# Second output projection in column halves, with the router and half of the first gather issued under and behind it; two small tables turned elsewhere

## The reference

```
h = rms_norm(x);  q,k,v,qi,ki,wi,pool,gate_a,gate_p = split(h @ w_in)      # 1024 x 3652
attn = top-64 sparse attention chosen by the indexer (qi, ki, wi), rotary, softmax
pooled = multi-scale trailing means minus identity, mixed per group, scaled
merged = sigmoid(gate_a) * (attn @ w_branch_attn) + sigmoid(gate_p) * (pooled @ w_branch_pool)
x = x + merged @ w_out
h2 = rms_norm(x);  logits = h2 @ router_w + router_b;  top 4 of 32 experts, softmax over the four
x = x + sum over chosen experts of gate * (swiglu(h2 @ w_gate_up[e] + b_gate_up[e]) @ w_down[e] + b_down[e])
```

## Time and profile before

| | |
|---|---|
| time, three runs | 1159.08, 1159.86, 1162.68 us; median 1159.86 |
| the profiled execution | 1162.73 us, its span 1160.8 us |
| PE busy | 1061.9 us (91%) |
| DVE, ACT busy | 291.2 us (25%), 117.4 us (10%) |
| DMA | 430.31 MB, mean 371 GB/s |

### The profile page before, as it was taken

The page is one execution under the profiler, slowest core; times in us unless marked ns, Lnnn a source line. Parts: engine busy times, 40 slices in busy tenths (PEclk is TensorE's granted clock), DMA queues, the critical chain, the costliest instruction groups (busy, mean ns, idle before and its releaser), DMA issues.

```text
span 1160.8 us, 12090 instructions
## 1 busy us (share of the span) xinstructions
PE 1061.9 (91%) x4830; PEld 442.6 (38%) x4830; DVE 291.2 (25%) x594; ACT 117.4 (10%) x208; POOL 5.2 (0%) x12
## 2 busy tenths in 40 slices
PE   7999999899999998989899999999999999999996
PEld 4544545543434342424243333333333333334332
DVE  2563121322222222121212122222222222222222
ACT  2124201110000101010100000000000000000000
POOL 1000000000000000000000000000000000000000
PEclk9899999899999999999999999999999999999999
DMA  9932475357999999999999999999999999999994
GB/s 348 340 141 73 167 278 206 137 235 298 430 427 427 431 427 430 427 430 428 429 429 427 430 427 430 427 429 429 427 430 427 430 427 430 428 429 429 427 423 184
DMA packets 39984, 430.31 MB, mean 371 GB/s; under 512 B 4880, under 2 KB 5008, under 8 KB 15392
## 3 DMA queue, kind: packets, MB, share of 16 engines
q1 hardware_dynamic: 39136, 428.11, 88.3%
q0 software_dynamic: 544, 1.90, 0.5%
q10 hardware_dynamic: 288, 0.08, 0.0%
HBM read 429.03 MB, written 1.05 MB: 370 GB/s over the span
## 4 chain that ended last, share of the span: by engine, by line
PE 65%; DMA 29%; DVE 3%; issue 1%; SPq 1%; ACT 0%; DVEq 0%
DMA slot<-w_gate_up_dram 28%; PE bank L1110 24%; PE bank L1135 11%; PE bank L862 9%; PE bank L1055 6%; PE bank L1084 5%; PE bank L889 5%; PE bank L1124 2%; DVE x L790 2%; PE bank L837 1%; PE bank L1095 1%; DMA slot<-w_down_dram 1%; PE bank L1026 0%; SPq L255 0%; DMA consts<-consts_dram 0%
## 5 line engine op out<-in xcount | busy, mean ns | idle before, releaser
L1110 PE MATMUL bank<-slot,scr 128*64 128x512 f32 x2048 | 461.6, 598 | 29.9 <-DMA slot<-w_gate_up_dram 29.9
L1110 PEld LDWEIGHTS bank<-slot,scr 128*64 128x64 f32 x2048 | 142.1, 137 | 319.6 <-issue 265.6
L1135 PE MATMUL bank<-slot,scr 128*64 128x512 f32 x1024 | 234.6, 600 | 20.3 <-DMA slot<-w_down_dram 19.2
L765 DVE COPY scr<-bank 128x512 f32<-128x512 f32 x32 | 22.1, 692 | 462.4 <-PE bank L1110 462.4
L1135 PEld LDWEIGHTS bank<-slot,scr 128*64 128x64 f32 x1024 | 69.8, 137 | 159.4 <-issue 120.8
L862 PE MATMUL bank<-slot,scr 128*128 128x512 f32 (+1 forms) x256 | 106.6, 578 | 2.1 <-DVE g L514 0.9
L1084 PE MATMUL bank<-scr 64*128 64x512 f32 x256 | 63.6, 613 | 24.3 <-DVE x L790 23.4
L790 DVE TENSOR_TENSOR x<-bank,x 128x512 f32<-128x512 f32 x68 | 44.0, 687 | 130.4 <-PE bank L1084 128.2
L862 PEld LDWEIGHTS bank<-slot,scr 128*128 128x128 f32 x256 | 48.3, 204 | 55.4 <-issue 53.2
L771 DVE TENSOR_TENSOR scr<-bank,bgu 128x512 f32<-128x512 f32 x64 | 41.2, 686 | 111.3 <-PE bank L1124 111.3
L1055 PEld LDWEIGHTS bank<-scr,xn 128*128 128x128 f32 x512 | 62.8, 199 | 13.2 <-issue 13.2
(11 more groups left out here) (166 smaller groups left out, 356.7 us busy)
## 6 DMA issues: line engine op xcount, KB each, us to landing
slot<-w_gate_up_dram SPq DMA_DIRECT2D x128, 2048.0 KB, 32.8
slot<-w_down_dram SPq DMA_DIRECT2D x64, 2048.0 KB, 21.1
slot<-w_in_dram SPq DMA_DIRECT2D x14, 1024.0 KB, 15.3
slot<-w_out_dram SPq DMA_DIRECT2D x4, 1024.0 KB, 4.8
slot<-w_branch_attn_dram SPq DMA_DIRECT2D x2, 1024.0 KB, 9.2
slot<-w_branch_pool_dram SPq DMA_DIRECT2D x2, 1024.0 KB, 5.0
x<-x_dram SPq DMA_DIRECT2D x2, 512.0 KB, 5.8
out_dram<-x SPq DMA_DIRECT2D x4, 256.0 KB, 2.1
```

The source lines that it names most:

```text
L765: V.tensor_copy(gu_sb[:, 512:1024], GB[1][:, :]).then_inc(gu_copied[1], 1)
L1110: ins = MM(GB[h][T * g:T * g + T, :], xgT[:, k, T * e:T * e + T], gu_slot[s][:, c0:c0 + 512], start=k == 0, stop=k == KC - 1)
L1135: ins = MM(DB[T * h:T * h + T, :], actT[e][:, c, :], v3(dn_slot[j][:, :], 4)[:, k, 512 * h:512 * h + 512], start=c == 0, stop=c == KC - 1)
```

## The change

- `turn_tables` leaves its place after group 0. The gain `g2` is now fetched in its final order straight from memory by four DMAs of 256 single numbers each on POOL's queue. The bias table is turned by `turn_biases`, after chunk 5 of the first `gate_up`, through the bank DB; DVE copies it back just before the first `swiglu`. `gates_turned` moves from chunk 2 to chunk 3.
- PE no longer waits for its own `job_ready` after each projection or branch: SP waits for `job_ready` itself (`unit_free`).
- Block 1 of `w_out` is done by column halves: first h=0 over all chunks, then h=1. Under it stand the turn and router of block 0, the turn of the first half of block 1 and block 0's ranks.
- Behind it the turn of the second half of block 1 and block 1's router (in two halves) are mixed with block 0's share of the first gather (`gather_first`); block 1's share follows after its ranks (`gather_rest`). Block 0's half of the selection is made early (`first_sel(0)`), block 1's after its ranks. Block 1's hT now overwrites block 0's columns. The sum of counts is waited for after the selection, from the bank TU[0].

The diff, cut to its core:

```diff
-            0, 4, 5, 6, 7, 9, 11, 25, 29, 13, 15, 19, 21, 27, 31, (35, 39), (37, 41), (38, 42))
+            0, 4, 5, 6, 7, 9, 11, 25, 29, 13, 15, 19, 21, 27, 31, ((35, 36), (38, 40)), (37, 41), (39, 42))
...
         def _(sp):
...
+            def unit_free(u):
+                if u < 16 and u % 2 == 1:
+                    sp.wait_ge(job_ready, u + 1)
+                elif u in LAST_OF_BRANCH:
+                    sp.wait_ge(job_ready, LAST_OF_BRANCH[u])
+                else:
+                    sp.wait_ge(unit_used[u % HALVES], u // HALVES + 1 if u % 2 == 0 else 1)
             def pre_unit(u):
...
-                    sp.wait_ge(unit_used[s], u // HALVES)
+                    unit_free(u - HALVES)
...
+            for k in range(2):
+                for m in range(2):
+                    pool_e.dma_start(g2_t[64 * m:64 * m + 64, k:KC:2],
+                                     cols_d[k:P:2, P_G2 + m:P_G2 + KC:2], allow_slow_non_contiguous=True).then_inc(g2_in, 16)
...
-                act.wait_ge(x2_ready, b + 1)
+                act.wait_ge(x2_ready, 2 * b + 2)
...
-            dve.wait_ge(turned_ready, 1)
-            V.tensor_copy(bgu_t[:, :].rearrange("p (e j k g) -> p e j k g", e=E, j=2, k=4),
-                          bank[4][:, :].rearrange("p (k e j g) -> p e j k g", k=4, e=E, j=2)).then_inc(turned_read, 1)
-            V.tensor_copy(g2_t[:, :].rearrange("p (j k) -> p j k", k=2), bank[5][:, 0:KC].rearrange("p (k j) -> p j k", k=2)).then_inc(turned_read, 1)
-            dve.wait_ge(turned_read, 2)
...
-            def residual(b):
+            def residual(b, h):
...
-                for h in range(2):
-                    dve.wait_ge(job_ready, 2 * j + 1 + h)
-                    V.tensor_tensor(x[:, b, 512 * h:512 * h + 512], bank[PAIR_BANKS[j % 3][h]][:, :],
-                                    x[:, b, 512 * h:512 * h + 512], ALU.add).then_inc(job_read, 1)
-                dve.wait_ge(job_read, 2 * j + 2)
+                dve.wait_ge(job_ready, 2 * j + 1 + h)
+                V.tensor_tensor(x[:, b, 512 * h:512 * h + 512], bank[PAIR_BANKS[j % 3][h]][:, :],
+                                x[:, b, 512 * h:512 * h + 512], ALU.add).then_inc(job_read, 1)
+                dve.wait_ge(job_read, 2 * j + 1 + h)
...
-                for g in range(2):
-                    gained(TJ_H2[b] + g, 4 * g, b, P_G2)
...
-            residual(0)
+            residual(0, 0)
+            residual(0, 1)
+            for g in range(2):
+                gained(TJ_H2[0][g], 4 * g, 0, P_G2)
...
+            residual(1, 0)
+            gained(TJ_H2[1][0], 0, 0, P_G2)
...
-            V.tensor_tensor(rank[:, 0, :], TB[j % 2][:, 0:E], notm[:, 0, :], ALU.add)
+            step(V.tensor_tensor(rank[:, 0, :], TB[j % 2][:, 0:E], notm[:, 0, :], ALU.add))
...
-            residual(1)
+            def first_sel(b):
+                r = rank[:, b, 0:2].unsqueeze(2).to_broadcast([P, 2, T])
+                V.tensor_tensor(sel[:, b, :, :], iota.unsqueeze(1).to_broadcast([P, 2, T]), r, ALU.is_equal).then_inc(sel_ready, 1)
+            first_sel(0)
+            residual(1, 1)
+            gained(TJ_H2[1][1], 4, 0, P_G2)
...
-            step(V.tensor_tensor(rank[:, 1, :], TB[j % 2][:, 0:E], notm[:, 1, :], ALU.add))
+            V.tensor_tensor(rank[:, 1, :], TB[j % 2][:, 0:E], notm[:, 1, :], ALU.add).then_inc(t_read[j % 2], 1)
+            dve.wait_ge(t_read[j % 2], j // 2 + 1)
+            first_sel(1)
...
-            make_sel(0)
-            V.tensor_tensor(first_cnt, TB[j % 2][:, P:P + E], first_cnt, ALU.add).then_inc(t_read[j % 2], 1)
-            dve.wait_ge(t_read[j % 2], j // 2 + 1)
+            dve.wait_ge(count_ready, 1)
+            V.tensor_tensor(first_cnt, TU[0][:, 0:E], first_cnt, ALU.add).then_inc(count_read, 1)
+            dve.wait_ge(count_read, 1)
...
-                    scale_gates(after, q1, q4, q)
...
+            dve.wait_ge(g2_in, 64)
...
+            dve.wait_ge(turned_ready, 1)
+            V.tensor_copy(bgu_t[:, :].rearrange("p (e j k g) -> p e j k g", e=E, j=2, k=4),
+                          DB[:, :].rearrange("p (k e j g) -> p e j k g", k=4, e=E, j=2)).then_inc(turned_read, 1)
+            dve.wait_ge(turned_read, 1)
...
-                    if half == 1:
-                        pe.wait_ge(job_ready, 2 * j + 2)
-                        pe.sem_inc(unit_used[u % HALVES], 1)
...
             def branch(b, j0, u0, nk, lhs, between=()):
...
-                if b == NB - 1:
-                    pe.wait_ge(job_ready, 2 * (j0 + NB))
-                    pe.sem_inc(unit_used[(u0 + nk // 2 - 1) % HALVES], 1)
...
-            def turn_tables():
+            def turn_biases():
...
-                pe.wait_ge(cols_in, 16)
...
-                        MM(bank[4][32 * g:32 * g + 32, k * P:k * P + P], ident[:, k::4],
-                           bgu_t[:, :].rearrange("p (e j c g) -> p e j c g", e=E, j=2, c=4)[:, :, :, g, :],
-                           start=True, stop=True)
-                for k in range(2):
-                    for g in range(2):
-                        ins = MM(bank[5][64 * g:64 * g + 64, 4 * k:4 * k + 4], ident[:, k::2], cols[:, P_G2 + g:P_G2 + g + 7:2],
+                        ins = MM(DB[32 * g:32 * g + 32, k * P:k * P + P], ident[:, k::4],
+                                 bgu_t[:, :].rearrange("p (e j c g) -> p e j c g", e=E, j=2, c=4)[:, :, :, g, :],
...
-                pe.wait_ge(turned_read, 2)
...
-            turn_tables()
...
-            def turn_x2(b):
-                pe.wait_ge(x2_ready, b + 1)
-                for g in range(2):
-                    transposes(TJ_H2[b] + g, [x[:, b, (4 * g + k) * P:(4 * g + k + 1) * P] for k in range(4)])
+            def turn_x2(b, halves):
+                for g in halves:
+                    pe.wait_ge(x2_ready, 2 * b + g + 1)
+                    transposes(TJ_H2[b][g], [x[:, b, (4 * g + k) * P:(4 * g + k + 1) * P] for k in range(4)])
...
-            def router(b):
+            def router(b, halves):
...
-                dst = t_job(TJ_R[b])
-                short_read(pe, TJ_H2[b] + 2)
-                for k in range(KC):
-                    ins = MM(dst[:, 0:E], hT[:, k, b * P:b * P + P], rw[:, k, :], start=k == 0, stop=k == KC - 1)
-                ins.then_inc(t_ready, 1)
+                j = TJ_R[b]
+                for g in halves:
+                    if g == 0:
+                        pe.wait_ge(t_read[j % 2], j // 2)
+                    else:
+                        t_job(j)
+                    pe.wait_ge(t_read[TJ_H2[b][g] % 2], TJ_H2[b][g] // 2 + 1)
+                    for k in range(4 * g, 4 * g + 4):
+                        ins = MM(TB[j % 2][:, 0:E], hT[:, k, 0:P], rw[:, k, :], start=k == 0, stop=k == KC - 1)
+                if g == 1:
+                    ins.then_inc(t_ready, 1)
...
-                MM(dst[:, 0:E], tri, msk[:, b, :], start=True, stop=True)
-                MM(dst[:, P:P + E], ones, msk[:, b, :], start=True, stop=True).then_inc(t_ready, 1)
+                if b == 0:
+                    MM(dst[:, 0:E], tri, msk[:, b, :], start=True, stop=True)
+                    MM(dst[:, P:P + E], ones, msk[:, b, :], start=True, stop=True).then_inc(t_ready, 1)
+                else:
+                    MM(dst[:, 0:E], tri, msk[:, b, :], start=True, stop=True).then_inc(t_ready, 1)
+                    MM(TU[0][:, 0:E], ones, msk[:, b, :], start=True, stop=True).then_inc(count_ready, 1)
+            def gather_first(h):
+                pe.wait_ge(sel_ready, 1)
+                pe.wait_ge(xn_ready, 2 * NB)
+                for k in range(4):
+                    c0 = (4 * h + k) // 2 * 2 * P + k % 2
+                    MM(XY[h][:, k * P:k * P + P], xn[:, 0, c0:c0 + 2 * P - 1:2], selb[:, 0:P], start=k == 0, stop=False)
+            def gather_rest():
+                pe.wait_ge(sel_ready, 2)
+                pe.wait_ge(xn_ready, 3 * NB)
+                for h in range(2):
+                    for k in range(4):
+                        c0 = (4 * h + k) // 2 * 2 * P + k % 2
+                        ins = MM(XY[h][:, k * P:k * P + P], xn[:, 1, c0:c0 + 2 * P - 1:2], selb[:, P:2 * P], start=False, stop=k == 3)
+                    ins.then_inc(done[f"X{h}"], 1)
...
-            branch(1, BJ_WO, 20, 8, hT, ((2, lambda: turn_x2(0)), (4, lambda: router(0))))
-            ranks(0)
-            turn_x2(1)
-            router(1)
+            free_banks(BJ_WO + 1)
+            for h in range(2):
+                for k in range(KC):
+                    if h == 0 and k == 4:
+                        turn_x2(0, (0, 1))
+                    if h == 1 and k == 0:
+                        router(0, (0, 1))
+                    if h == 1 and k == 3:
+                        turn_x2(1, (0,))
+                    if h == 1 and k == 6:
+                        ranks(0)
+                    u = 20 + k // 2
+                    ins = MM(bank[PAIR_BANKS[(BJ_WO + 1) % 3][h]][:, :], hT[:, k, P:2 * P],
```

(57 more changed lines are left out.)

## The result

Four executions each: before 1159.47 us median (1158.02 to 1162.68), the changed kernel 1147.46 us (1145.3 to 1150.18). The ratio is 0.9894 with a 95% interval of 0.9861 to 0.9927, so 12 us less. The profiled execution took 1149.2 us, span 1147.4.

What follows compares the result with a forecast made beforehand. Bound: PE's path to the down-slot issue T0 (267.8), then a fixed 893 us. Gains 2.7 + 4.0 + 2.2 + 8.2 - 1.3 = 15.8 us gave 1146.9 from the profiled execution, 1144.0 from the median; forecast 1145, range 1141 to 1151.

Steps and rivals of the forecast that it cites:

- What bounds it: Whole kernel: PE's gains before the down-slot issue after the DMA hole count in full, later ones nothing; 893 us follow.
- T0: SP's next issue of expert 0's down slots after the DMA hole, at 267.8 us before the change.
- rival D: Expert stream is bound by bandwidth, so an earlier PE only waits earlier: no change, 1160 us; chance 0.04.
- Early part: Groups 0 to 2: without tables group 1 starts 2.7 us earlier, and the clock staying up gives 4.0.
- The clock's 4.0: Groups 1 and 2: clock stays up without tables and wait, 5.58-3.0 and 15.38-14.0, together 4.0 us.
- PE's waits for itself: Behind projections and branches: eight more waits of 0.29 us removed, part returned at ACT's waits; 2.2 us gained.
- Rival B: Clock at 1.2 GHz after all, in group 1 (4.0) or the end's mixed work (3.4): 1148.5 to 1149; chance 0.27.
- New DMAs: Four DMAs of 256 four-byte numbers on POOL's queue, sharing engines with w_in: cost nothing, bound 0 to 3.0 us.
- rival E: Slower: the 1024 four-byte pieces clog the 16 engines ahead of w_in's units, 1174 us at 600 ns each; chance 0.04.
- End: End of the dense part: overlapped turns, router and gather start gate_up at 214.7 instead of 222.95, 8.2 us gained.
- Biases: In gate_up: 32 records turning the bias table now lie on the path before the down-slot issue, costing 1.3 us.
- rival C: Early lead lost: behind the indexer or softmax PE waits for DVE or ACT, 2.7+4.0 given back, 1151.7; chance 0.10.

## Why the prediction was right

The time of 1147.46 us lies 2.5 above the forecast of 1145 and inside its range of 1141 to 1151. The mechanism was right, and most terms were; two of the terms were off in opposite ways, so that the nearness of the sum is in part luck.

**What bounds it.** Right, and this carried the rest. In all thirteen profiles the span is T0 plus 891.6 to 894.8 us. An earlier PE was never hidden by the stream (rival D).

**Early part.** 7.0 against 7.3, and the tables' return cost 5.9. Of the 2.7 us that went, about 1.5 was the table products, which only moved: the sum had their 1.3 in gate_up as its own term. The net gain was the wait and the clock behind it. The clock's 4.0 was somewhat large: group 1 took 3.77 at full clock where PE's waits were back, about 3.6 in the changed kernel (43.07 less 12.02 and two groups of 13.74), not 3.0.

**PE's waits for itself.** Mis-sized: 2.2 forecast for eight of them, and with the two that stood in other terms (0.29 each) 2.8 for ten; about 4.5 measured for all eleven. I had read only the idle row and not the overlap of records that is lost on both sides of it. This went unseen in the sum because the next point took it back.

**The clock.** The forecast had it up at group 1 and at the end: both right in all three profiles of the changed kernel. What the sum lacked were the indexer and the softmax: 3.3 us there in the first profile. Rival B named the mechanism, at two other places, and a price of 3.4 to 4.0 us. The executions of the changed kernel fall into two sorts: over its three sets those with a mean clock of 0.997 or more took 1143.8 to 1145.7 us, those with 0.996 or less 1147.4 to 1150.2. The forecast of 1145 is the first sort, the median of 1147.5 lies between. Why the clock fell at these two places and had not before is open; that PE's waits for itself are gone is one candidate (above). The lower end of the range, 1141, does not follow from the terms that the prediction names for it: 1144.0 less 0.2 and 1.7 is 1142.1.

**New DMAs.** They cost the path nothing, as said: the four DMAs took POOL 2.47 us, landed in 7.7 (median; the row used for the forecast had 3.0), and PE ran groups 0 to 3 without a gap. The Trainium skill, "DMA: Bandwidth & Descriptors" (Specifications), has transfers below 512 bytes fall short of line rate; no cost of that to the path shows here (rival E).

**End.** 9.1 against 9.3, and 0.9 against 1.1 ahead of it: step for step. What I did not foresee is that the clock hangs on `gather_first`: 3.9 us without it, in place of the 1.0 to 1.6 that I expected for its hidden work.

**Biases.** 1.35 against 1.3. The lead was kept through DVE and ACT (rival C): 108.7 us from group 3 to w_out in the profile at full clock, where PE's waits for itself made it 111.4, just as before.

## What to carry to other kernels

When a prefetch fills all buffers and then stops, find the first issue after the hole: in this kernel the time was that moment plus a constant, and only work ahead of it counted. Ask of each wait on TensorE what it does to the clock afterwards: here a wait of 0.8 us between thin products went with 4.3 us, five times its length, in one profile against another. Useful products (the biases) and useless ones (the fillers) put into such waits cost no time here. A wait of TensorE for its own last result cost up to 0.53 us where its idle row shows 0.29, since the overlap with the next record is lost as well.

## What the runs showed of the hardware that I had not expected

- The clock fell although PE was busy. The four bias products (32 rows of the array, 512 columns, 3.88 us for eight records) were followed by a low stretch in seven of thirteen profiles, and the 16 records of gate_up behind them then took 5.28 instead of 3.58 us. In two more the clock fell already during them, and the two pieces took 4.7 and 6.1.
- The same program has three such low stretches before T0 in one execution and none in another (1149.2 and 1144.65 us), with starts of the first long piece 1.4 us apart.
- A group of 512-column products with nothing directly behind it is 0.24 us longer in its own row, beside the 0.29 that shows as a wait.
